# A two-block transformer on one core: the high and low activation halves in one 512-column product where there are 256 tokens

## The reference

```python
def swiglu(h, w_gate, w_up, w_down):           # FFN = 2816 hidden channels
    return (jax.nn.silu(h @ w_gate) * (h @ w_up)) @ w_down

def half_ffn(t, m, j):                         # first block, twice in each layer
    h = modulate(rmsnorm(t, norm_g[l, j]), m[3 * j], m[3 * j + 1])
    return t + 0.5 * m[3 * j + 2] * swiglu(h, ffn_w_gate[l, j // 2], ffn_w_up[l, j // 2],
                                          ffn_w_down[l, j // 2])
# first block, layer 0: Fourier mixer; layer 1: retention mixer, (silu(g) * yn) @ w_out
# the context is dropped after layer 1's mixer: from there on there are 256 tokens, not 512
# second block, both layers:
x = x + 0.5 * swiglu_2(rmsnorm_2(x, ffn1_norm[l]), ffn1_w_in[l], ffn1_w_out[l])
x = x + merged @ w_out[l]                      # merged: a recurrent and an attention branch, gated
x = x + 0.5 * swiglu_2(rmsnorm_2(x, ffn2_norm[l]), ffn2_w_in[l], ffn2_w_out[l])
```

## Time and profile before

| | |
|---|---|
| median of 3 runs | 3546.66 us |
| the profiled execution | 3541.26 us |
| its span | 3539.5 us |
| TensorE busy (matmul / weight load) | 3431.8 us (97%) / 3109.0 us (88%) |
| VectorE busy | 2032.4 us (57%) |
| ScalarE busy | 1268.4 us (36%) |
| GpSimd busy | 640.2 us (18%) |
| DMA | 507.89 MB, mean 143 GB/s |

### The profile page before, as it was taken

One profiled execution on the slowest core, in us unless ns is written; L12 is line 12 of the kernel. 1 busy time (PEld: TensorE's weight loads), 2 busy tenths in 40 slices (PEclk: granted clock), 3 DMA queues, 4 the chain that ended last, 5 costly groups with the idle time before them and its releaser, 6 DMA issues.

```text
span 3539.5 us, 55525 instructions
## 1 busy us (share of the span) xinstructions
PE 3431.8 (97%) x22315; PEld 3109.0 (88%) x22315; DVE 2032.4 (57%) x2374; ACT 1268.4 (36%) x1678; POOL 640.2 (18%) x535
## 2 busy tenths in 40 slices
PE   7999999999999999999999999999999999998999
PEld 4888878888888888888999999989999999998999
DVE  3766836657766535545555456855545455864644
ACT  2222223212232124333434344355444444355443
POOL 2212303202221130002222220000323230000222
PEclk9999999999999999999999999999999999999999
DMA  5645504545355433334654654334565655343664
GB/s 195 189 149 155 161 22 123 173 140 175 107 172 167 130 97 89 90 95 140 184 173 140 182 166 138 108 114 131 158 183 165 184 167 155 108 120 93 177 184 143
DMA packets 862994, 507.89 MB, mean 143 GB/s; under 512 B 15060, under 2 KB 843024, under 8 KB 862800
## 3 DMA queue, kind: packets, MB, share of 16 engines
q1 hardware_dynamic: 862432, 503.74, 48.7%
q0 software_dynamic: 368, 1.38, 0.1%
HBM read 504.01 MB, written 1.05 MB: 143 GB/s over the span
## 4 chain that ended last, share of the span: by engine, by line
PE 87%; DVE 5%; ACT 4%; issue 2%; DMA 1%; POOL 0%; SPq 0%; DVEq 0%; POOLq 0%; ACTq 0%
PE bank L578 26%; PE bank L580 25%; PE bank L579 25%; ACT whi_all L1023 2%; PE bank L946 2%; PE bank L589 1%; DVE wlo_all L1271 1%; DVE t_full L1406 1%; PE bank L661 1%; PE bank L800 1%; PE bank L761 1%; PE bank L748 1%; PE bank L850 1%; PE bank L845 1%; DMA raw<-in_w_branch_a 1%
## 5 line engine op out<-in xcount | busy, mean ns | idle before, releaser
L1271 DVE TENSOR_TENSOR wlo_all<-raw,whi_all 128x1024 fp32r<-128x1024 f32 (+3 forms) x768 | 1015.1, 1323 | 972.1 <-ACT whi_all L1023 970.8
L578 PE MATMUL bank<-xn_hi,whi_all 128*128 128x256 f32 (+1 forms) x4608 | 1481.2, 321 | 18.6 <-DVE xn_lo L1395 11.4
L579 PE MATMUL bank<-xn_lo,whi_all 128*128 128x256 f32 (+1 forms) x4608 | 1447.4, 314 | 0.0
L580 PE MATMUL bank<-xn_hi,wlo_all 128*128 128x256 f32 (+1 forms) x4608 | 1447.2, 314 | 0.0
L1023 ACT CAST whi_all<-raw 128x1024 fp32r<-128x1024 f32 (+3 forms) x768 | 836.5, 1090 | 1032.6 <-PE bank L580 988.4
L578 PEld LDWEIGHTS bank<-xn_hi,whi_all 128*128 128x128 f32 x4608 | 882.6, 192 | 83.6 <-DVE xn_lo L1395 13.5
L580 PEld LDWEIGHTS bank<-xn_hi,wlo_all 128*128 128x128 f32 x4608 | 881.8, 191 | 52.3
L579 PEld LDWEIGHTS bank<-xn_lo,whi_all 128*128 128x128 f32 x4608 | 883.0, 192 | 49.5
L578 PE MATMUL bank<-h_hi,whi_all 128*128 128x256 f32 (+1 forms) x1408 | 459.0, 326 | 1.2 <-POOL h_lo L1767 1.2
L580 PE MATMUL bank<-h_hi,wlo_all 128*128 128x256 f32 (+1 forms) x1408 | 454.7, 323 | 0.0
L579 PE MATMUL bank<-h_lo,whi_all 128*128 128x256 f32 (+1 forms) x1408 | 454.4, 323 | 0.0
(11 more groups left out here) (247 smaller groups left out, 2802.2 us busy)
## 6 DMA issues: line engine op xcount, KB each, us to landing
raw<-in_ffn_w_in SPq DMA_DIRECT2D x176, 512.0 KB, 3.9
raw<-in_w_in SPq DMA_DIRECT2D x168, 512.0 KB, 3.8
ada_w<-in_ada_w SPq DMA_DIRECT2D x128, 512.0 KB, 4.0
raw<-in_ffn_w_gate SPq DMA_DIRECT2D x88, 512.0 KB, 3.8
raw<-in_ffn_w_up SPq DMA_DIRECT2D x88, 512.0 KB, 3.9
raw<-in_ffn_w_down SPq DMA_DIRECT2D x32, 768.0 KB, 5.2
raw<-in_ret_w_in SPq DMA_DIRECT2D x48, 512.0 KB, 3.8
raw<-in_ffn_w_out SPq DMA_DIRECT2D x32, 768.0 KB, 5.4
```

Of the source, the lines that this page charges most:

```text
L578: pe.matmul(o, whi[s][:, k, :], hi, start=(k == 0), stop=False)
L579: pe.matmul(o, whi[s][:, k, :], lo, start=False, stop=False)
L580: return pe.matmul(o, wlo[s][:, k, :], hi, start=False, stop=(k == ks - 1))
L1271: tt(wlo[s][:, 0:ks, :], raw[s][:, 0:ks, :], whi[s][:, 0:ks, :].bitcast(F32), ALU.subtract).then_inc(lo_done[s], 1)
```

## The change

Where there are 256 tokens (the five FFNs, `ret_out` and `wout`), the high and low activations lie in one tensor with an index for the half, and the two products by the high weights become one matmul of 512 columns. It writes high weights by high activations into the left half of the bank and high weights by low activations into the right half. The third product is added to the left half. Who reads the bank adds the two halves. The other phases of 256 tokens (`ret_g`, the mixer's input products, `br_a`, `br_b`) are left as they were.

```diff
+        def folded(a):
+            return a["T"] == SEQ
...
-            def block_mm(s, k, ks, T, hi, lo):
+            def block_mm(s, k, ks, T, hi, lo, two=None):
                 o = bank[s][:, 0:T]
+                if two is not None:
+                    both = bank[s][:].rearrange("p (c t) -> p c t", c=2)
+                    if k == 0:
+                        pe.matmul(both, whi[s][:, k, :], two, start=True, stop=False)
+                    mm = pe.matmul(o, wlo[s][:, k, :], hi, start=False, stop=False)
+                    if k:
+                        mm = pe.matmul(both, whi[s][:, k, :], two, start=False, stop=(k == ks - 1))
+                    return mm
                 pe.matmul(o, whi[s][:, k, :], hi, start=(k == 0), stop=False)
                 pe.matmul(o, whi[s][:, k, :], lo, start=False, stop=False)
                 return pe.matmul(o, wlo[s][:, k, :], hi, start=False, stop=(k == ks - 1))
...
                     def gate(it, s, r):                                  # ScalarE
-                        if s % 2 == 0:
+                        if s % 2 == 0 and folded(a):
+                            p = s // 2
+                            act.wait_ge(h_done[p], it + (q0 + 1))
+                            act.wait_ge(bank_free[s], r + 2)
+                            act.activation(silu_g[p][:, 0:T], silu_g[p][:, SEQ:2 * SEQ], ACT.Silu).then_inc(g_act[p], 1)
+                        elif s % 2 == 0:
                             act.wait_ge(h_done[s // 2], it + (q0 + 1))
                             act.activation(silu_g[s // 2][:, 0:T], bank[s][:, 0:T], ACT.Silu).then_inc(bank_free[s], 1)
...
             def residual(xt, s, k, T, gate):                             # VectorE
+                if T == SEQ:
+                    link(stt(xt[:, k, 0:SEQ], bank[s][:, SEQ:2 * SEQ], gate(k, 0), xt[:, k, 0:SEQ], ALU.mult, ALU.add))
+                    link.after()
+                    stt(xt[:, k, 0:SEQ], bank[s][:, 0:SEQ], gate(k, 0), xt[:, k, 0:SEQ], ALU.mult,
+                        ALU.add).then_inc(bank_free[s], 1)
+                    return
...
                     def times_up(it, s, r):                              # VectorE
-                        if s % 2:
+                        if folded(a):
+                            p, n = s // 2, it + folded_rounds(a, half)
+                            two = bank[s][:].rearrange("p (c t) -> p t c", c=2)
+                            if s % 2 == 0:
+                                dve.tensor_reduce(silu_g[p][:, SEQ:2 * SEQ], two, AXX, ALU.add).then_inc(bank_free[s], 1)
+                                return
+                            up = square[:, p * SEQ:(p + 1) * SEQ]
+                            dve.wait_ge(h_full[p], n + 1)
+                            dve.tensor_reduce(up, two, AXX, ALU.add).then_inc(bank_free[s], 1)
+                            dve.wait_ge(bank_free[s], r + 2)
+                            dve.wait_ge(g_act[p], n + 1)
+                            tt(silu_g[p][:, 0:T], silu_g[p][:, 0:T], up, ALU.mult).then_inc(h_full[p], 1)
+                        elif s % 2:
```

More of the change, by code:

```diff
@@ L309, in build @@
         x = at("x", [P, DC, 512], 0)
[L310 to L313, removed]
+        xn_two = at("xn_two", [P, 2, DC, 512], 16, F32R)
+        xn_hi, xn_lo = xn_two[:, 0], xn_two[:, 1]
+        h_two = at("h_two", [P, 2, KMAX, 512], 48, F32R)
+        h_hi, h_lo = h_two[:, 0], h_two[:, 1]
         t_full = at("t_full", [P, DC, 512], 48)
@@ L397, in build @@
         h_done = [sem(f"h_done{p}") for p in range(2)]
+        g_act = [sem(f"g_act{p}") for p in range(2)]
+        h_full = [sem(f"h_full{p}") for p in range(2)]
         in_sem = sem("in_sem")
@@ L728, in do_ffn @@
             def do_ffn(a):
-                hi, lo = (h2_hi, h2_lo) if a["mod"] is None else (h_hi, h_lo)
-                moving, ready = normed(a["norm"])
+                two = h2_two if a["mod"] is None else h_two
+                moving, ready = normed(a["norm"], folded(a))
                 for half in range(2):
@@ L734, in do_ffn @@
                     q0 = gu_rounds(a["f"], half)
-                    linear(f"{a['tag']}dn{half}", pair(hi, lo, a["T"]), a["T"],
+                    linear(f"{a['tag']}dn{half}", pair(two, a["T"], folded(a)), a["T"],
                            lambda k: [(h_done[k % 2], q0 + k // 2 + 2)])
@@ L811, in do_retention @@
                 pe.wait_ge(rt["zlo"], RH)
-                linear("ret_out", lambda s, k: (z_hi[:, 8 * (s % 2) + k, :], z_lo[:, 8 * (s % 2) + k, :]), SEQ)
+                halves = [pair(z_two[:, :, 8 * i:8 * i + 8], SEQ, True) for i in range(2)]
+                linear("ret_out", lambda s, k: halves[s % 2](s, k), SEQ)
             def do_mixer(a):
@@ L816, in do_mixer @@
                 moving, ready = normed(a["norm"])
-                attended = pair(ob_hi, ob_lo, SEQ)
+                attended = pair(ob_two, SEQ)
                 def unit(ph, it, s):
@@ L995, in do_mixer @@
                        lambda k: [(hg["olo"], 4 * l + k // 2 + 1)])
-                linear(f"wout{l}", pair(m_hi, m_lo, SEQ), SEQ, lambda k: [(hg["mlo"], DC * l + k + 1)])
+                linear(f"wout{l}", pair(m_two, SEQ, True), SEQ, lambda k: [(hg["mlo"], DC * l + k + 1)])
             do = dict(first=do_first, norm=do_norm, ffn=do_ffn, fourier=do_fourier,
@@ L1762, in do_ffn @@
                         for p in range(2):
-                            pool.wait_ge(bank_free[2 * p + 1], it + (ph["first"] + 2))
+                            if folded(a):
+                                pool.wait_ge(h_full[p], it + (folded_rounds(a, half) + 2))
+                            else:
+                                pool.wait_ge(bank_free[2 * p + 1], it + (ph["first"] + 2))
                             full = silu_g[p][:, 0:T].unsqueeze(1)
```

42 lines of the change are left out of this document (24 added, 18 removed).

## The result

The changed kernel is slower: 3563.2 us median (3560.6 to 3568.2, 4 runs) against 3545.2 (3542.8 to 3550.4, 4 runs) of the kernel before in the same session. The ratio is 1.0051, 95% interval [1.0033, 1.0068]: 18 us lost, where the forecast had 10.6 us gained and the range ended at 3560.

What follows compares the result with a forecast made beforehand. TensorE, busy 97% of the span, was taken as the bound. FFNs 34.3 - 25.5 = 8.8, plus 3.3 for `ret_out` and `wout`, less 0.7, 0.3 and 0.5: 10.6 us gained, forecast 3536.1 us, range 3512 to 3560.

Steps and rivals of the forecast that it cites:

- What bounds the kernel now: TensorE, busy 97% of the span; the seam between gate/up and down has no slack, so lateness there is lost in full.
- What is removed: In 256-token FFNs, `ret_out` and `wout`, one matmul's 13.0 ns beyond its columns saved per k-step: 37.6 us at most.
- Rival B: The 13 ns go with the columns, 512 columns take 240 ns, nothing is saved and seams still cost: 3567 us; chance 0.05.
- C: More gain than forecast: short matmuls pay no fee, k-step 0.330 us, about 3507; or seams cost nothing, 3510; chance 0.11.
- What is added: VectorE's bank reduce in gate and up, 0.68 us; a pair of units takes 5.45 us against TensorE's 5.55, so hidden there.
- Rival A: VectorE sets the pace of gate and up: reduce of 0.80 us gives 3551, 0.90 gives 3573; chance 0.20.
- The seams: Between gate/up and down, late `h_lo` adds 3.1 us in first halves and 2.0 in second, over five FFNs: 25.5 us.
- The table of the forecast: Last gate/up round, first half, VectorE's times for units 0 to 3 from t = 0; `h_lo` near 15.15, wanted at 12.1.
- VectorE lies up to a unit behind: In gate and up, VectorE may lag TensorE by up to a unit, while a slot has three units' time.
- 25.5 us are given back: Loss from added seam waits in the five FFNs, 5 x (3.1 + 2.0), subtracted from the FFNs' 34.3 us.
- Small terms: Second residual `stt`: 0.3 us in all ahead of norms, and 0.5 us for TensorE's wait at the very end.

Runs made afterwards that it cites:

- e1: Changed kernel's folded matmuls with the bank readers of the kernel before, right half left out of the result; 3520.8 us, ratio 0.9935 to the kernel before.
- e2: The three matmuls of the kernel before with the changed kernel's readers, which sum both bank halves; 3577.5 us, ratio 1.0095 to the kernel before.
- e5: Changed kernel plus 16 (first halves) and 10 (second halves) dummy 128-column matmuls ahead of TensorE's h wait; 3541.5 us, ratio 0.9985 to the kernel before.
- e6: Changed kernel plus 8 (first halves) and 5 (second halves) dummy 128-column matmuls ahead of TensorE's h wait; 3546.5 us, ratio 1.0002 to the kernel before.
- e4: Changed kernel with ScalarE casting the next weights ahead of silu in folded gate/up units; 3522.7 us, ratio 0.9948 to the kernel before.
- e3: Changed kernel plus 28 (first halves) and 18 (second halves) dummy 128-column matmuls ahead of TensorE's h wait; 3561.0 us, ratio 1.0050 to the kernel before.

## Why the prediction was wrong

- **"What bounds the kernel now": right.** TensorE bounds it, and the seam has no slack; e1 and e2 show both. 
- **"What is removed", 13.0 ns a k-step: the term was too large.** Measured 10, so 29.0 us instead of 37.6. The step added two paces that were each read in a stream of one size, and one of them over 22 starts only. This took 8.6 us off the gain. Rival B (nothing saved) and C's 0.330 us are both out. The Trainium skill ("TensorE: Matmul & The Clock Gate", section "Back-to-back issue gap") gives N/2.4 GHz + 2.5 ns for a warm clock. It calls this the gap of an isolated matmul, which in a stream with weight loads comes out too short at small N and too long at large N; the prediction used it for such a stream without saying so. Used that way it is an estimate of 325 ns for this k-step. The trace has 349 to 350, and the formula is too short at both sizes here: 109 against 119.9 ns and 216 against 226.8.
- **"What is added": right for VectorE.** Reduce 0.685 (0.68), multiply 0.425 (0.41), silu 0.42 (0.41), split 1.267 (1.255). Rival A did not come about: there is no wait for `lo_done` in gate and up.
- **The seams, 25.5 us: too small by 3.3.** The first halves wait up to 3.64 us (3.1 forecast), the second about 2.4 (2.2); the total grew by 28.8. In the first seam GpSimd's cast began 0.18 behind the multiply's end and ended 0.26 behind the split's (forecast 0.17 and 0.31), so the links at its end held. The lateness was there from the start. The table of the forecast lets VectorE reduce unit 0 at t = 0. TensorE began the next unit at 1738.47, and the reduce began at 1739.16, behind the split of the unit before: 0.6 us of backlog, which the forecast itself had named ("VectorE lies up to a unit behind") and then not carried into the table. Another link was off: silu follows the reduce by 0.12 us (1739.16 + 0.68 to 1739.96), not by 0.03, and there are two of these in the round.
- **The step that failed: the sum counted a wait at its length.** `25.5 us are given back` prices a wait inside a 256-token FFN as idle time and nothing else. The clock drops to half behind it, for some 3.4 us. e5 keeps the waits and takes only the fall away: 23 us, with 16 to 30 possible. The budget leaves 16 for it, and the granted clocks of the runs give 17. Without this term the change would have been level, within what a measurement tells; with it, it is slower.
- **Small terms.** Forecast were 0.3 for the norms and 0.5 for the end. The norms' waits did not grow, the end cost its 0.5, and the wait for `m_two` in `wout`, which the forecast did not have, cost 1.1.
- The forecast's error is 10.6 + 18 = 28.6 us: 8.6 from the matmul's term, 3.3 from the waits for h, 0.8 from the small terms, and some 16 from the clock.

No rival had this mechanism. The slower ones (A, B) ended at the right time for reasons that the runs refute.

## What to carry to other kernels

A new wait on TensorE is to be priced at its length plus what the clock takes behind it, and the trace before shows both beside its own waits: here 3.6 us of idle cost 5.1. A pace is to be read over hundreds of instructions, in the mix that the changed kernel will have. And when a fold moves work to an engine that is idle for 43% of the span, look at the order of its neighbours first: putting ScalarE's cast ahead of silu turned 18 us lost into 19 gained, with no instruction removed.

## What the runs showed of the hardware

- Of ten TensorE waits of 2.4 to 3.6 us (the change), nine had a stretch at clock 0.50 begin in or just behind them, 3.4 us long in eight cases and 6.8 in one. Of ten waits of 2.0 to 2.9 us (e2) it was nine too, of five of 1.9 us (e6) two, of five of 1.2 us (e6) none, and of ten of at most 0.9 us (e4) none.
- The 58 runs of the kernel before spread over 18 us. Most of that goes with their mean granted clock (0.987 to 0.992): without its part the spread is 7.5 us.
- Each 128-column fp32 filler shows as two matmuls and takes 0.22 us (6.17 us for 28 in e3), more than a 256-column fp32r one with 0.12.
- A k-step of one 512- and one 256-column matmul takes 349 to 350 ns where streams of one size have 226.8 and 119.9. Units of eight alternate between 2.78 and 2.81 us when the sizes alternate, and last 2.79 when they are grouped.
- GpSimd's 256-column operations last 0.40 us (cast) and 0.72 to 0.75 (subtraction) alone, and until the end of the split when VectorE runs one beside them: 1.75 and 1.80 for the cast, 1.64 for the subtraction.
